# Local attentions with three banks for turned maps, q and k rotated in the scan, and three smaller moves

## The reference

```
layer 0 mixer:  differential attention (4 double heads)  +  neighbourhood attention (8 heads)
layer 1 mixer:  window attention with a sink (8 heads, 2 key heads)  +  a state-space scan in both directions

apply_rope(u):  out[2i] = u[2i]*cos - u[2i+1]*sin;  out[2i+1] = u[2i]*sin + u[2i+1]*cos
dtf = softplus(dt_raw + dt_bias);   a = -exp(a_log);   cum = cumsum(dt * a) in chunks of 128
carry = carry * exp(last) + states;   y = y_diag + y_off
y = (y + d_skip * xs) * silu(z);   y = y * rsqrt(mean(y*y) + eps) * gnorm_g
gate, idx = top_k(softmax(h @ w_router) of each expert, 2 * n / 16)
out = out.at[idx].add(ffn(h[idx]) * gate)
x = x + gate2 * rmsnorm(moe, g_post)
```

## Time and profile before

| what | value |
|---|---|
| runs of the kernel before | 3862.12, 3866.82, 3867.98 us, median 3866.82 |
| profiled execution, its own time | 3870.88 us |
| its span | 3869.1 us |
| mean granted clock of PE | 0.944 |
| PE busy | 3438.4 us, 89% |
| PE weight loads busy | 2349.5 us, 61% |
| DVE busy | 1162.4 us, 30% |
| ACT busy | 921.1 us, 24% |
| POOL busy | 491.0 us, 13% |

### The profile page before, as it was taken

How to read it: one execution, slowest core, us unless ns; L and a number is a source line. 1 busy time by engine, 2 the same in 40 slices (tenths; PEclk the granted TensorE clock), 3 DMA queues, 4 the chain that set the end, 5 groups by cost and what they waited for, 6 DMA issues and landing times. The chain is left out here.

```text
span 3869.1 us, 51564 instructions
## 1 busy us (share of the span) xinstructions
PE 3438.4 (89%) x19840; PEld 2349.5 (61%) x19840; DVE 1162.4 (30%) x2735; ACT 921.1 (24%) x2084; POOL 491.0 (13%) x628
## 2 busy tenths in 40 slices
PE   6999989969998399999999689698799579999994
PEld 2444445545544377888778565565564368788873
DVE  1000167646622411101111143455672421011112
ACT  3100156634523011111111132343352211111111
POOL 0000124010000011111001230113300000000003
PEclk8999999989999699999999889899899789999997
DMA  6327355443032677877778630101303478998885
GB/s 209 109 97 116 102 172 175 142 115 120 1 118 96 228 249 250 275 246 260 252 250 275 196 127 1 47 4 45 82 1 108 144 265 310 322 318 305 314 318 208
DMA packets 379802, 674.34 MB, mean 174 GB/s; under 512 B 80144, under 2 KB 118208, under 8 KB 373376
## 3 DMA queue, kind: packets, MB, share of 16 engines
q1 hardware_dynamic: 343360, 543.69, 41.6%
q10 hardware_dynamic: 22864, 82.06, 5.8%
q0 software_dynamic: 13440, 46.80, 5.0%
HBM read 586.86 MB, written 91.83 MB: 175 GB/s over the span
## 5 line engine op out<-in xcount | busy, mean ns | idle before, releaser
L2133 PE MATMUL experts_gu_ps<-experts_xT,experts_wg 128*128 128x160 f32 (+1 forms) x4096 | 552.5, 288 | 4.5 <-DVE experts_xT L2062 2.5
L2133 PE MATMUL experts_gu_ps<-experts_xT,experts_wu 128*128 128x160 f32 (+1 forms) x4096 | 549.3, 287 | 0.0
L2133 PEld LDWEIGHTS experts_gu_ps<-experts_xT,experts_wg 128*128 128x128 f32 x4096 | 529.7, 192 | 19.3 <-issue 19.3
L2133 PEld LDWEIGHTS experts_gu_ps<-experts_xT,experts_wu 128*128 128x128 f32 x4096 | 524.8, 191 | 0.0
L2104 PE MATMUL experts_y_ps<-experts_wd,experts_hid 128*128 128x512 f32 x1024 | 452.3, 597 | 0.0
L515 PE MATMUL proj_pb_ps<-proj_ahead_w,proj_hT 128*128 128x512 f32 x960 | 415.6, 594 | 0.0
L2075 DVE TENSOR_TENSOR experts_hid<-experts_sil,experts_gu_ps 128x160 f32<-128x160 f32 (+1 forms) x256 | 78.0, 305 | 941.5 <-ACT experts_sil L2039 937.5
L2039 ACT ACTIVATE experts_sil<-experts_gu_ps 128x160 f32<-128x160 f32 (+1 forms) x256 | 74.5, 291 | 1106.6 <-PE experts_gu_ps L2133 1106.6
L2104 PEld LDWEIGHTS experts_y_ps<-experts_wd,experts_hid 128*128 128x128 f32 x1024 | 190.6, 190 | 231.3 <-issue 228.5
L515 PEld LDWEIGHTS proj_pb_ps<-proj_ahead_w,proj_hT 128*128 128x128 f32 x960 | 181.9, 191 | 223.7 <-issue 223.7
L2011 POOL DMA_INDIRECT moe<-experts_y,experts_ixs x32 | 51.2, 1601 | 1131.7 <-DVE experts_y L2079 1131.7
(11 more groups left out here) (381 smaller groups left out, 4270.5 us busy)
## 6 DMA issues: line engine op xcount, KB each, us to landing
experts_wg<-in_l_w_gate SPq DMA_DIRECT2D x64, 2048.0 KB, 8.4
experts_wu<-in_l_w_up SPq DMA_DIRECT2D x64, 2048.0 KB, 13.6
experts_wd<-in_l_w_down SPq DMA_DIRECT2D x64, 2048.0 KB, 11.4
attn_a_mod_w<-in_l_w_mod ACTq DMA_DIRECT2D x36, 1024.0 KB, 4.9
proj<-proj_ob ACTq DMA_DIRECT2D x60, 256.0 KB, 2.1
proj_ahead_w<-in_l_w_in SPq DMA_DIRECT2D x6, 2048.0 KB, 9.8
attn_near_bias<-lines SPq DMA_DIRECT2D x80, 128.0 KB, 2.8
mix_xr<-res SPq DMA_DIRECT2D x18, 512.0 KB, 3.8
```

The costliest lines, as they stand in the source:

```text
L2133: mm = nc.tensor.matmul(GU[f % 2][:, part, 0:N], w[:, h, k, c * P:(c + 1) * P], xT[:, k, :], start=(k == 0), stop=(k == KD - 1))
```

## The change

1. Local attentions: T has three banks, and the outputs of two items lie in the halves of one. PE scores both chunks of the item ahead, turns up to three rounds and then weighs; a fourth round is turned after the second weighing. The reciprocal is made on one column per head and then copied to 128 columns. DVE does the previous item's output first, ahead of the scores. ACT does the factor's copy and one exponent ahead of its rounds.
2. The band attention has no rotations; it loads queries and keys that are rotated already. `scan` rotates them: SP loads the keys and the cosines and sines of a tile beside the projected queries, POOL rotates the 640 columns in six instructions of 320, ACT stores them. `FILLS` alternates q and z and ends with the last q. The weights of z and q are loaded first, then skip and norm vectors, then the tiles of keys.
3. The rates and triangles of the scan are made in `front`, between the last keys and the first channel; `FrontAhead` loads the two vectors of each direction. PE's two waits at the scan's start are gone, and DVE waits for the cleared carry in the first two steps.
4. `Choice.select` makes the indices first and signals `chosen`, then the weights and signals `weighed`.
5. In `finish` POOL makes only the roots, and DVE does all products and additions.

```diff
+  r = st.sb("r", [P, 4, 2])
+  rw = st.sb("rw", [P, 4, 2, HD])
   S = [[st.ps(f"s{s}{m}", [P, BANK]) for m in range(2)] for s in range(2)]
-  T = [st.ps(f"tr{s}", [P, 4, P]) for s in range(2)]
-  O = [st.ps(f"o{s}", [P, BANK]) for s in range(2)]
...
+  T = [st.ps(f"tr{s}", [P, 4, P]) for s in range(3)]
+  O = st.ps("o", [P, 2, 2, P])
...
+     load_qk(0)
      sp.dma_start(k[0][:], rows[:, :, K0:K0 + P]).then_inc(k_in[0], 16)
-     sp.dma_start(cos[:], rope[0].rearrange("(t p) n -> p t n", p=P)).then_inc(const_in, 16)
-     sp.dma_start(sin[:], rope[1].rearrange("(t p) n -> p t n", p=P)).then_inc(const_in, 16)
-     load_qk(0)
      sp.dma_start(sink[:], sinks.rearrange("(a h j) -> a h j", a=1, h=2).broadcast_to([P, 2, PAIRS])).then_inc(const_in, 16)
...
-
-     def rotate(i):
-      pool.wait_ge(q_in[i % 2], START + 32 * (i // 2 + 1))
-      if i >= 1:
-       pool.wait_ge(t_done, START + (prepared(i - 1) if i >= 2 else len(Q_PREP)))
-      rotate_pairs(nc.gpsimd, link, q[i % 2], qr, cos, sin, t1, t2)
-      pool.sem_inc(q_ready, 1)
...
-     rotate(0)
      for n in range(ITEMS):
       sink_column(n)
-      if n % NQ == 0 and n // NQ + 1 < PAIRS:
-       rotate(n // NQ + 1)
...
     for n in range(ITEMS):
      ahead = n + AHEAD - 1
      waiting = [m for m in range(2) if ahead < ITEMS]
+     if n >= 1:
+      turned_factor(n - 1)
+     if waiting:
+      exp(ahead, waiting.pop(0))
      for j in range(len(rounds(n % NQ))):
       if (turn_at[n] + j) % 2 == 0:
        turned(act, n, j)
...
-     if n >= 1:
-      turned_factor(n - 1)
...
-     nc.vector.reciprocal(r[:, n % 4, :, :], sums[:, n % SLOTS, :].unsqueeze(2).to_broadcast([P, 2, HD])).then_inc(r_done, 1)
+     nc.vector.reciprocal(r[:, n % 4, :], sums[:, n % SLOTS, :]).then_inc(r_done, 1)
+     dve.wait_ge(r_done, START + n + 1)
+     nc.vector.tensor_copy(rw[:, n % 4], r[:, n % 4, :].unsqueeze(2).to_broadcast([P, 2, HD])).then_inc(rw_done, 1)
...
-     dve.wait_ge(const_in, START + 48)
-     dve.wait_ge(k_in[0], START + 16)
-     rotate_pairs(nc.vector, link, k[0], kr, cos, sin, t3, t4)
-     dve.sem_inc(k_ready, 1)
...
+     if n >= 1:
+      output(n - 1)
...
-     if n >= 1:
-      output(n - 1)
...
-     if at >= 2:
-      pe.wait_ge(t_out[at % 2], START + at // 2)
+     if at >= 3:
+      pe.wait_ge(t_out[(at - 3) % 2], START + (at - 3) // 2 + 1)
...
+     if j == 0 and n >= 1:
+      pe.wait_ge(o_out, START + n)
...
+      pe.wait_ge(rw_done, START + n + 1)
+      nc.tensor.transpose(O[:, n % 2, 1, :], rw[:, n % 4].rearrange("p m c -> p (m c)"), K.ident[:]).then_inc(o_done, 1)
...
      todo = list(range(len(chunks(ahead % NQ)))) if ahead < ITEMS else []
      turns = len(rounds(n % NQ))
-     if todo:
-      score(ahead, todo.pop(0))
-     turn_round(n, 0)
-     if todo:
-      score(ahead, todo.pop(0))
-     for j in range(1, turns):
+     for j in todo:
+      score(ahead, j)
+     for j in range(min(turns, 3)):
       turn_round(n, j)
-      weigh_values(n, j - 1)
+     for j in range(turns - 1):
+      weigh_values(n, j)
+      if j == 1 and turns > 3:
+       turn_round(n, 3)
      for which, tiles in prep_of(n):
       prepare(n // NQ + 1, which, tiles, turn_at[n + 1] - 1)
      weigh_values(n, turns - 1)
...
-  t = self.t
-  for n, (turn, group) in enumerate([(0, 0), (1, 1), (2, 0), (3, 1)] + ([(1, 2), (3, 2)] if self.with_ctx else [])):
-   link(nc.vector.tensor_copy(t[:, n, :], self.bank[:, turn, self.lane(group)]))
-  link(nc.vector.tensor_tensor(self.first[:], t[:, 0, :], t[:, 1, :], ALU.is_ge))
-  link(nc.vector.tensor_scalar(t[:, 3, :], t[:, 3, :], float(self.HALF), None, ALU.add))
-  link(nc.vector.tensor_tensor(self.weight[:, 0:E], t[:, 0, :], t[:, 1, :], ALU.max))
-  link(nc.vector.tensor_tensor(t[:, 2, :], t[:, 2, :], t[:, 3, :], ALU.subtract))
+  t, bank = self.t, self.bank
+  first, second = self.lane(0), self.lane(1)
+  link(nc.vector.tensor_copy(t[:, 0, :], bank[:, 1, second]))
+  link(nc.vector.tensor_tensor(self.first[:], bank[:, 0, first], t[:, 0, :], ALU.is_ge))
+  link(nc.vector.tensor_scalar(t[:, 1, :], bank[:, 3, second], float(self.HALF), None, ALU.add))
+  link(nc.vector.tensor_tensor(t[:, 2, :], bank[:, 2, first], t[:, 1, :], ALU.subtract))
   link(nc.vector.tensor_tensor(t[:, 2, :], t[:, 2, :], self.first[:], ALU.mult))
-  link(nc.vector.tensor_tensor(self.index[:, 0:E], t[:, 2, :], t[:, 3, :], ALU.add))
+  link(nc.vector.tensor_tensor(self.index[:, 0:E], t[:, 2, :], t[:, 1, :], ALU.add))
+  if self.with_ctx:
+   link(nc.vector.tensor_scalar(t[:, 5, :], bank[:, 3, self.lane(2)], float(SEQ), None, ALU.add))
+   link(nc.vector.tensor_copy(self.index_c[:, 0:E], t[:, 5, :]))
+  dve.sem_inc(self.chosen, 1)
+  link(nc.vector.tensor_tensor(self.weight[:, 0:E], bank[:, 0, first], t[:, 0, :], ALU.max))
...
+   link(nc.vector.tensor_copy(self.weight_c[:, 0:E], bank[:, 1, self.lane(2)]))
...
-  dve.sem_inc(self.chosen, 1)
+  dve.sem_inc(self.weighed, 1)
...
+  for d in range(2):
+   sp.dma_start(self.alog[:, d * HEADS_D:(d + 1) * HEADS_D], row(self.a_logs[d], HEADS_D)).then_inc(self.rate_in, 16)
+   sp.dma_start(self.dtb[:, d * HEADS_D:(d + 1) * HEADS_D], row(self.dt_biases[d], HEADS_D)).then_inc(self.rate_in, 16)
...
     pool.wait_ge(choice.chosen, START + 1)
     gather(0)
+    pool.wait_ge(choice.weighed, START + 1)
...
     choice.turn(pe)
+    pe.wait_ge(choice.weighed, START + 1)
     turn_rows(0)
...
-     sp.wait_ge(xv_done, START + t // 2 + 1)
+     sp.wait_ge(x_done, START + t + 1)
...
-    pool.wait_ge(x_in, START + 16 * NTX)
-    rsqrt(0)
-    rsqrt(1)
     for t in range(NTX):
-     if t + 2 < NTX:
-      rsqrt(t + 2)
-     if t % 2 == 1:
-      pool.wait_ge(m_done, START + t + 1)
-      nc.gpsimd.tensor_tensor(x[:, t, :], m[:, t, :], x[:, t, :], ALU.add).then_inc(xp_done, 1)
+     rsqrt(t)
...
      dve.wait_ge(rs_done, START + t + 1)
      nc.vector.scalar_tensor_tensor(m[:, t, :], m[:, t, :], ms[:, t:t + 1], gate[:], ALU.mult, ALU.mult).then_inc(m_done, 1)
-     if t % 2 == 0:
-      dve.wait_ge(m_done, START + t + 1)
-      nc.vector.tensor_tensor(x[:, t, :], m[:, t, :], x[:, t, :], ALU.add).then_inc(xv_done, 1)
+     dve.wait_ge(m_done, START + t + 1)
+     nc.vector.tensor_tensor(x[:, t, :], m[:, t, :], x[:, t, :], ALU.add).then_inc(x_done, 1)
...
+    link(nc.gpsimd.memset(tri[:], 1.0))
+    link(nc.gpsimd.affine_select(out=tri[:, 0, :], in_=tri[:, 0, :], compare_op=ALU.is_ge, fill=0.0, base=0,
...
+    act.wait_ge(sp1, START + 1)
+    nc.scalar.activation(sp_a[:], sp_a[:], ACT.Exp, scale=-1.0).then_inc(sp2, 1)
+    nc.scalar.activation(alog[:], alog[:], ACT.Exp).then_inc(sp2, 1)
+    act.wait_ge(sp2, START + 2)
+    nc.scalar.activation(sp_a[:], sp_a[:], ACT.Ln, bias=1.0).then_inc(sp2, 1)
...
+    per_tile = lambda v: v.unsqueeze(1).to_broadcast([P, NT, 2 * HEADS_D])
+    dve.wait_ge(rate_in, START + 16 * 4)
+    dve.wait_ge(kv_out, START + NT)
+    link(nc.vector.tensor_tensor(dt[:], dt[:], per_tile(dtb[:]), ALU.add))
+    link(nc.vector.tensor_scalar(sp_b[:], dt[:], -1.0, None, ALU.mult))
+    nc.vector.tensor_tensor(sp_a[:], dt[:], sp_b[:], ALU.max).then_inc(sp1, 1)
+    dve.wait_ge(sp1, START + 1)
+    link(nc.vector.tensor_scalar(sp_b[:], dt[:], 0.0, None, ALU.max))
+    dve.wait_ge(sp2, START + 3)
+    link(nc.vector.tensor_tensor(dt[:], sp_b[:], sp_a[:], ALU.add))
+    link(nc.vector.tensor_scalar(alog[:], alog[:], -1.0, None, ALU.mult))
+    link(nc.vector.tensor_tensor(da[:], dt[:], per_tile(alog[:]), ALU.mult))
...
- FILLS = [("z", t) for t in (3, 4, 2, 5, 1, 6, 0, 7)] + [("q", t) for t in range(NTX)]
+ Z_ORDER = (3, 4, 2, 5, 1, 6, 0, 7)
+ FILLS = [fill for j, t in enumerate(Z_ORDER[:7]) for fill in (("q", j), ("z", t))] + [("z", Z_ORDER[7]), ("q", 7)]
...
-    for d in range(2):
-     sp.dma_start(alog[:, d * H8:(d + 1) * H8], row(a_logs[d], H8)).then_inc(const_in, 16)
-     sp.dma_start(dtb[:, d * H8:(d + 1) * H8], row(dt_biases[d], H8)).then_inc(const_in, 16)
+    def load_k(t):
+
+     rows = slice(t * P, (t + 1) * P)
+     if t >= 2:
+      sp.wait_ge(q_out[t % 2], START + 16 * (t // 2))
+     sp.dma_start(qk[:, t % 2, BANK:QK], proj[rows, BANK:QK]).then_inc(k_in[t % 2], 16)
+     sp.dma_start(cos[:, t % 2, :], rope[0][rows, :]).then_inc(k_in[t % 2], 16)
+     sp.dma_start(sin[:, t % 2, :], rope[1][rows, :]).then_inc(k_in[t % 2], 16)
+
+    for s, first in ((1, 0), (0, Z0)):
+     sp.dma_start(w[:, s], w_rows[:, :, first:first + BANK]).then_inc(w_sem[s], 16)
     sp.dma_start(skip[:], row(d_skip, H8)).then_inc(const_in, 16)
     sp.dma_start(gn[:], row(gnorm_g, INNER)).then_inc(const_in, 16)
-    for s, first in enumerate((Z0, 0)):
-     sp.dma_start(w[:, s], w_rows[:, :, first:first + BANK]).then_inc(w_sem[s], 16)
+    for t in range(5):
+     load_k(t)
     for j, t in enumerate(order):
      sp.wait_ge(o_done, START + j + 1)
      sp.dma_start(out[t * P:(t + 1) * P, INNER:2 * INNER], o[:, j % 2, :]).then_inc(o_out[j % 2], 16)
+     if j < 3:
+      load_k(5 + j)
...
```

(38 more changed lines are left out.)

134 lines of the change are left out of this document (51 added, 83 removed).

## The result

The changed kernel takes 3803.6 us in the median of four runs (3797.8 to 3810.5), the kernel before 3867.4; the ratio is 0.9836, with an interval of 0.982 to 0.9851. The profiled execution of the changed kernel took 3797.8 us with a span of 3796.0, against 3870.9 and 3869.1: 73.1 us to explain. The runs of the changed kernel spread over 13 us, and the longer ones have the lower mean clock (0.946 and not 0.951), so the profiled one is from the short end.

The account below looks back on a forecast made before the run. TensorE was taken as the bound inside nearly every stage, so only its waits counted, mostly at seams; terms summed to -32.7 us, giving 3838.2 against the profiled time and 3834.1 against the median, so 3836 us, range 3823 to 3854.

Parts of the forecast that it names:

- Local attentions: Near attention: three banks and new order cut TensorE's waits from 11.0 to 7.4 us, 3.6 us gained (9 gained to 6 lost).
- Band items: Band attention: short kind stays at 4.80 us, 12 longer ones fall from 5.54 to about 5.3, 2.5 us gained.
- The reciprocal: Both attentions: one-column reciprocal saves VectorE about 0.5 us in each of 72 items, but VectorE is not the bound.
- Output bank shared by two items: Both attentions: first weighing waits for the previous output, which VectorE does first in about 0.7 us; cost nothing.
- Head of the scan: Scan's start: first product 15.1 us earlier, 3.5 lost as GpSimd's skip-vector products collide with VectorE; net 11.6 us gained.
- Body of the scan: Scan's steps: GpSimd's rotation fits steps of 12.84 us but delays VectorE's products; 1.5 us lost (0 to 12).
- first rival: Scan becomes bound by its chain of VectorE and ScalarE, 2.5 us in each of seven rotations: 3853 us; chance 0.17.
- Tail and head of the band attention: Last query tile's rotation unhidden at scan's end, 5.6 us lost; band attention's first scores 13 us in, 15 gained.
- Last stage: All products and additions on VectorE, eight tiles of 2.61 us: 20.9 us, 5.1 us gained (3.5 to 6).
- Front: Rates made in the front hide in ScalarE's idle 14.35 us: cost 0, or 4 if the cover were gone.
- The second: Rival: all near waits go, scan-head collision falls into waits, band head starts earlier, 7 + 4 + 3: 3822 us; chance 0.15.
- The third and fourth: Rivals: VectorE's output first holds score banks, 3886 us, chance 0.05; three banks leave TensorE's waits, 3842 us, chance 0.06.

Follow-up runs that it names:

- one_tile_size: The changed kernel with weighing on all 128 columns of the values for each head (128*128 tiles, that part of the result not computed); single run 3851.9 us.
- order_back: The changed kernel with only TensorE's old order inside an item put back (score, turn, score, turn, weigh, turn, weigh); 3827.35 us, 0.9897 of before.
- rates_only: The kernel before with only the rates, the triangles and PE's waits moved as in the change; 3858.4 us, ratio 0.9972 to before.

## Why the prediction was wrong, step by step

- *Local attentions.* Here it failed. The step is the sentence that laid out an item "by hand from durations of the same kinds": I took TensorE's work as a constant and let only waits move. The durations of the earlier trace rows were those of runs of one kind, each with the charge of a change in it, and the order removes four of them per item. The term was put at nothing without a reason; put back alone, the order cost 14.6 us in the near attention and 11.9 in the band attention, of the 35 that the attentions gained. With 0.12 to 0.15 us by 4 by 64 items, 31 to 38 us, the kernel's time would have come out at 3798 to 3805 us, but partly by luck: with the 6.1 us that I had priced for waits, the attentions alone would have had 37 to 44 us of gain for the measured 34.8. The waits of the near attention that the view counts fell by 2.0 us for the 3.6 that I had summed. The context items took 0.55 us longer for the first of a pair and 0.26 less for the second, where I had said 0.8 longer.
- *Band items.* Predicted 4.80 and 5.3, measured 4.34 and 5.11. The wait in the long kind did not fall, 0.59 us before and 0.72 after: VectorE's copy of round 0 still comes behind two scores.
- *The reciprocal.* That VectorE "is not the bound" is false of the new order: with the wide reciprocal the near item takes 0.44 us more. In the old order it was not tested alone; the near item there fell from 6.75 to 6.44 us with the short reciprocal, the third bank and the output first together.
- *Output bank shared by two items, priced at nothing.* Right: no wait on it shows.
- *Head of the scan* right in the wait (15.1, 15.2). The collision with GpSimd's products was real, a VectorE product took 1.31 us in place of 0.69, but TensorE's waits in the whole scan grew only by some 1.4 us; 3.5 was too much.
- *Body of the scan, first rival.* I priced 1.5 us, and head and body together lost 1.6 for the 5.0 that I had summed; the first rival did not come. GpSimd's rotation instructions took 0.86 to 1.40 us, and VectorE's products beside them became longer, yet each step took 12.84 us. The slack of 2.9 us was still 2.7. The rule of the Trainium skill that the prediction names ("SBUF — State Buffer", section "Who interferes with whom") is seen in these durations and not in the sum.
- *Tail and head of the band attention* right: 6.1 for 5.6, 16.3 for 15.
- *Last stage* right: from the first product to the last addition's end 20.3 us for 20.9.
- *Front.* Priced at 0 and gave 5.1, by the clock; whether the change brought it is open. I had looked for work that moves and not for a stage at the edge between two clock patterns.
- *Rivals.* The second, more gained than priced, came nearest with 3822 but by another mechanism. The third and fourth did not come.

The range failed because its ends were made of waits alone; a term that I had held fixed had no bound at all.

## What to carry to other kernels

When TensorE's work is short and of several shapes, count the changes of array shape in the loop, price one from the starts of a long and a short run of the same instruction, and group the work; then look what the grouping uncovers, since copies that a change of kind had covered become waits, and another bank is what pays for that. An engine that had room beside the old order is not thereby free in the new one. Before an order is changed at a stage's end, list which tile each engine finishes last: the same move failed with one list and made the seam 5 us shorter with the other.

## What the runs showed of the hardware

- A change between 128*128 and 128*64 on the array cost about 0.15 us between instructions of 0.055 and 0.11 us, and the weight load idled 0.17 us at each; between instructions of the same shape both vanished, although one was a transpose and the other a product (one_tile_size). In an item without waits four changes cost 0.66 us (order_back).
- The front, which differs between kernels only by small added work, ran in 215 or 220 us as the clock stayed at its upper level or fell back to the lower one at gaps of TensorE of 3.0 us; before that point the traces differ by fractions of a microsecond.
- In rates_only the scan started 15 us earlier, and the granted clock in its first and third 12.8 us was 0.64 and 0.87 where it had been 0.83 and 1.00; about 5 of the 15 us were lost again. The changed kernel, as early, had 0.86 and 0.93.
- A reciprocal that VectorE spreads to 128 columns took 0.94 us; one of 2 columns took 0.15 and the copy to 128 columns 0.23.
